# First scores in other banks, HGRN sums and logarithms pair by pair, exponentials behind the first eviction, one eviction by VectorE

## The reference, cut to what matters

```python
def hgrn2_mixer(q, i, g, zf, zb, lb, norm_g):
    ...
    o = (o_f + o_b).transpose(0, 2, 1, 3)
    gate = jax.nn.silu(g.astype(jnp.float32)).reshape(B, S, HG_HEADS, HEAD_DIM)
    o = rms_norm(o, norm_g) * gate
    return o.reshape(B, S, HG_WIDTH).astype(q.dtype)

    def attend(q_blk):
        s = jnp.einsum('bkgqd,bksd->bkgqs', q_blk, kh) * scale
        p = jax.nn.softmax(s, axis=-1)
        return jnp.einsum('bkgqs,bksd->bkgqd', p, vh)
```

## Time and profile before

| what | us |
|---|---|
| median of 3 runs | 1583.99 (1583.55 to 1588.25) |
| profiled execution | 1584.87 |
| its span, first to last instruction | 1583.0 |
| TensorE busy (matmul) in the span | 1532.4 (97%) |
| VectorE, ScalarE, GpSimd busy | 622.1, 424.9, 377.3 |
| chain that ended last: TensorE, DMA, VectorE, ScalarE | 81%, 9%, 7%, 2% |

### The profile page before, as it was taken

How to read it: one execution, slowest core, us unless ns; L and a number is a source line. 1 busy time by engine, 2 the same in 40 slices (tenths; PEclk the granted TensorE clock), 3 DMA queues, 4 the chain that set the end, 5 groups by cost and what they waited for, 6 DMA issues and landing times.

```text
span 1583.0 us, 20229 instructions
## 1 busy us (share of the span) xinstructions
PE 1532.4 (97%) x8166; PEld 786.7 (50%) x8166; DVE 622.1 (39%) x1244; ACT 424.9 (27%) x762; POOL 377.3 (24%) x432
## 2 busy tenths in 40 slices
PE   8999999999999999998999999999999999999986
PEld 4655566555444444443347546755554444444432
DVE  2687546462122212211427965464622122113114
ACT  3654651211111111111235547403111111111102
POOL 4671790000000000000265637700000000000004
PEclk9999999999999999999999999999999999999999
DMA  9300403699999999999950003066999999999997
GB/s 393 147 0 14 147 1 87 265 382 423 428 425 428 427 426 427 426 426 429 384 228 1 1 28 134 1 183 265 386 425 428 425 427 427 426 428 427 427 425 296
DMA packets 57682, 470.02 MB, mean 297 GB/s; under 512 B 19385, under 2 KB 19513, under 8 KB 29394
## 3 DMA queue, kind: packets, MB, share of 16 engines
q1 hardware_dynamic: 50338, 452.37, 69.0%
q0 software_dynamic: 7104, 16.24, 2.7%
q10 hardware_dynamic: 144, 0.07, 0.0%
HBM read 447.69 MB, written 26.74 MB: 300 GB/s over the span
## 4 chain that ended last, share of the span: by engine, by line
PE 81%; DMA 9%; DVE 7%; ACT 2%; issue 1%; POOL 0%; SPq 0%; POOLq 0%; DVEq 0%
PE bank L1035 24%; PE bank L1072 11%; PE bank L659 10%; PE bank L1025 9%; PE bank L817 6%; DMA ring<-wu 5%; DMA hbuf<-wu 2%; PE bank L738 2%; PE bank L725 2%; PE bank L753 2%; PE bank L651 2%; PE bank L1012 1%; PE bank L1059 1%; DVE x L2046 1%; PE bank L645 1%
## 5 line engine op out<-in xcount | busy, mean ns | idle before, releaser
L2268 POOL DMA_INDIRECT expert_rows<-raw_qd,store_rows x60 | 58.8, 979 | 999.4 <-ACT raw_qd L1472 939.3
L1035 PE MATMUL bank<-ring,hbuf 128*64 128x512 f32 x640 | 281.3, 593 | 5.3 <-DMA ring<-wu 5.3
L1036 PE MATMUL bank<-ring,hbuf 128*64 128x512 f32 x640 | 281.5, 593 | 0.0
L2020 DVE COPY raw_qd<-bank 128x256 f32<-128x256 f32 x64 | 27.2, 425 | 637.7 <-PE bank L1059 637.7
L659 PE MATMUL bank<-hbuf,ring 128*128 128x512 f32 x480 | 210.8, 595 | 2.8 <-DVE hbuf L1535 2.8
L1035 PEld LDWEIGHTS bank<-ring,hbuf 128*64 128x64 f32 x640 | 86.7, 137 | 184.2 <-issue 184.2
L1035 PE MATMUL bank<-raw_qd,hbuf 128*64 128x512 f32 x372 | 165.4, 597 | 3.9 <-DMA hbuf<-wu 3.9
L1072 PE MATMUL bank<-ring,raw_qd 128*64 128x512 f32 x352 | 160.4, 598 | 3.1 <-DVE raw_qd L2020 3.1
L1074 PE MATMUL bank<-ring,raw_qd 128*64 128x512 f32 x352 | 160.4, 598 | 0.0
L1025 PE MATMUL bank<-raw_qd,x 128*128 128x192 f32 x896 | 159.5, 332 | 0.0
L1465 ACT ACTIVATE raw_qd<-bank 64x512 f32<-64x512 f32 x64 | 37.8, 590 | 417.3 <-PE bank L1036 417.3
(11 more groups left out here) (405 smaller groups left out, 2233.8 us busy)
## 6 DMA issues: line engine op xcount, KB each, us to landing
ring<-wd SPq DMA_DIRECT2D x40, 2048.0 KB, 19.0
ring<-wg SPq DMA_DIRECT2D x38, 2048.0 KB, 19.1
ring<-wu SPq DMA_DIRECT2D x36, 2048.0 KB, 21.9
ninth_slot<-wd SPq DMA_DIRECT2D x20, 2048.0 KB, 20.4
hbuf<-wu SPq DMA_DIRECT2D x18, 2048.0 KB, 23.9
raw_qd<-wg SPq DMA_DIRECT2D x18, 2048.0 KB, 19.4
ring<-w_in SPq DMA_DIRECT2D x6, 2048.0 KB, 18.8
raw_qd<-wg SPq DMA_DIRECT2D x6, 1792.0 KB, 12.6
```

The costliest lines, as they stand in the source:

```text
L1035: mm(pb[2 + par][0:CAP, :], tokens[:, k, :], gates[k], start=(k == 0), stop=(k == KT - 1))
L1036: last = mm(pb[2 + par][CAP:P, :], tokens[:, k, :], ups[k], start=(k == 0), stop=(k == KT - 1))
L2268: G.indirect_dma_start(out=half_rows, out_offset=bass.IndirectOffsetOnAxis(ap=store_i[:, e:e + 1], axis=0), in_=y_sb[e % 2], in_offset=Non ...
```

## The change

- `S_BANK` becomes (2, 0): even units have their scores in banks 2 and 3, odd ones in 0 and 1; the first group of the output projection goes to bank 2. `scores(0)` no longer waits for the evacuation of groups 24 and 25; `scores(1)` does.
- TensorE's order becomes `scores(0)`, `scores(1)`, `head_sums(0)`, `hgrn_out(1)`, `scores(2)`, `head_sums(1)`; the loop's first iteration has no scores.
- `pair_out` signals the square and the copy each. ScalarE takes the first pair's logarithm ahead of `pair_out(1)`, the second one's behind it. `turned(0)` waits for one logarithm per bank.
- Both exponentials for the roots move behind the eviction of unit 0.
- Both `head_norm` stand in VectorE's u = 1. At the end of that iteration VectorE evicts the transposed probabilities of unit 1 in place of ScalarE.

```diff
-        S_BANK, T_BANK, A_BANK = (0, 2), 4, (pb[6], pb[7])
-        EARLY_BANK = [pb[0], pb[6]] + [pb[6 + n % 2] for n in range(2, 2 * NB)]
+        S_BANK, T_BANK, A_BANK = (2, 0), 4, (pb[6], pb[7])
+        EARLY_BANK = [pb[2], pb[6]] + [pb[6 + n % 2] for n in range(2, 2 * NB)]
...
             def head_sums(p):
-                pe.wait_ge(s["ho_s"], on("ho_s") + p + 1)
+                pe.wait_ge(s["ho_s"], on("ho_s") + 2 * p + 1)
+                pe.wait_ge(s["kv_e"], on("kv_e") + HG)
...
                 if u == 0:
+                    pe.wait_ge(s["r_ln"], on("r_ln") + 5)
+                    pe.wait_ge(s["r_done"], on("r_done") + 5)
+                elif u == 1:
                     wait_evacuated(pe, layer, NG - 2)
                     wait_evacuated(pe, layer, NG - 1)
-                    pe.wait_ge(s["r_ln"], on("r_ln") + 5)
-                    pe.wait_ge(s["r_done"], on("r_done") + 5)
...
                 if u == 0:
-                    pe.wait_ge(s["ho_s"], on("ho_s") + 2)
-                    pe.wait_ge(s["ho_r"], on("ho_r") + 1)
                     pe.wait_ge(s["hs_m"], on("hs_m") + HG)
                 else:
                     pe.wait_ge(s["pt_e"], on("pt_e") + u)
                 for i in range(2):
+                    if u == 0:
+                        pe.wait_ge(s["ho_r"], on("ho_r") + i + 1)
...
                 if u >= 2:
                     pe.wait_ge(s["o_b"], on("o_b") + u - 1)
+                elif u == 1:
+                    pe.wait_ge(s["ho_s"], on("ho_s") + 4)
...
             scores(0)
             scores(1)
+            head_sums(0)
             hgrn_out(1)
-            head_sums(0)
+            scores(2)
             head_sums(1)
...
             for u in range(NU):
-                if u + 2 < NU:
+                if 0 < u < NU - 2:
                     scores(u + 2)
...
             def pair_out(p):
                 act.wait_ge(s["ho"], on("ho") + p + 1)
-                A(o_rs[p], O_BANK[:, :], ACT.Square)
+                A(o_rs[p], O_BANK[:, :], ACT.Square).then_inc(s["ho_s"], 1)
                 A(o_sb[p], O_BANK[:, :], ACT.Copy).then_inc(s["ho_s"], 1)
 
-            def head_rstd():
-                for p in range(2):
-                    act.wait_ge(s["ho_m"], on("ho_m") + p + 1)
-                    ins = A(o_rs[p], M_BANK[p][:, :], ACT.Ln, bias=eps, scale=1.0 / HD)
-                ins.then_inc(s["ho_r"], 1)
-                act.wait_ge(s["ho_r"], on("ho_r") + 1)
+            def head_log(p):
+                act.wait_ge(s["ho_m"], on("ho_m") + p + 1)
+                A(o_rs[p], M_BANK[p][:, :], ACT.Ln, bias=eps, scale=1.0 / HD).then_inc(s["ho_r"], 1)
+
+            def head_roots():
+                act.wait_ge(s["ho_r"], on("ho_r") + 2)
                 for p in range(2):
                     A(o_rs[p], o_rs[p], ACT.Exp, scale=-0.5).then_inc(s["ho_r"], 1)
...
             probs(0)
             probs(1)
+            head_log(0)
             pair_out(1)
-            head_rstd()
+            head_log(1)
             for u in range(NU):
-                act.wait_ge(s["pt"], on("pt") + u + 1)
-                if u >= 2:
-                    act.wait_ge(s["pv"], on("pv") + u - 1)
-                A(pT_sb[u % 2], banks[:, T_BANK:T_BANK + 2, :], ACT.Copy).then_inc(s["pt_e"], 1)
+                if u != BY_VECTOR:
+                    act.wait_ge(s["pt"], on("pt") + u + 1)
+                    if u >= 2:
+                        act.wait_ge(s["pv"], on("pv") + u - 1)
+                    A(pT_sb[u % 2], banks[:, T_BANK:T_BANK + 2, :], ACT.Copy).then_inc(s["pt_e"], 1)
+                if u == 0:
+                    head_roots()
                 if u + 2 < NU:
                     probs(u + 2)
...
-                if u in (1, 2):
-                    head_norm(u - 1)
+                if u == 1:
+                    head_norm(0)
+                    head_norm(1)
                 if u >= 1:
                     unit_out(u - 1)
+                if u == BY_VECTOR:
+                    dve.wait_ge(s["pt"], on("pt") + u + 1)
+                    V.tensor_copy(pT_sb[u % 2], banks[:, T_BANK:T_BANK + 2, :]).then_inc(s["pt_e"], 1)
```

More of the change, by code:

```diff
@@ L278, in trunk @@
             kv_e="ACT: chunk k v evacuated, after the decay rows", state="DVE: chunk states",
-            ho="PE: HGRN outputs of a pair of heads", ho_s="ACT: HGRN output of a pair, its squares",
-            ho_m="PE: HGRN square sums", ho_r="ACT: HGRN logarithms of both pairs, then rstd of each", o_a="DVE: o_a of a pair",
+            ho="PE: HGRN outputs of a pair of heads", ho_s="ACT: squares of the HGRN output of a pair, the output",
+            ho_m="PE: HGRN square sums", ho_r="ACT: HGRN logarithms of each pair, then rstd of each", o_a="DVE: o_a of a pair",
             qk="PE: attention scores", mx="DVE: row maxima",
             ex="ACT: probabilities", pn="DVE: inverse sums of a unit", pt="PE: probabilities transposed",
-            pt_e="ACT: transposed probabilities evacuated", pv="PE: attention output of a unit, inverse sums by row",
+            pt_e="ACT, once DVE: transposed probabilities evacuated", pv="PE: attention output of a unit, inverse sums by row",
             pn_e="DVE: inverse sums by row evacuated", o_b="DVE: o_b of a unit", u5="u stored, loaded by chunk, then S5 chunk matrix loaded",
@@ L311, in trunk @@
             ev_a=15, prep=3, h_e=4, act=2, h_s=4, sig_e=4, h_l=4, h_f=4, q_copy=8, r_sq=5, ke_e=4,
-            kv_e=4, r_ln=5, r_rs=5, ho_s=2, ex=16, ho_r=3, pt_e=16, bt_e=4, ke=8, y5_e=1, gx=4, h2_a=4,
+            kv_e=4, r_ln=5, r_rs=5, ho_s=4, ex=16, ho_r=4, pt_e=16, bt_e=4, ke=8, y5_e=1, gx=4, h2_a=4,
             rlT_e=4, rms2=1, gx2=2, ev_d=13, dve=161, lb=3, h_k=4, q_silu=4, h_c=4, head=4, r_y=5, hs_m=4,
@@ L412, in trunk @@
         NU = QH // 2 * NB
+        BY_VECTOR = 1
         target = {8: Z[0], 9: Z[1], 10: Z[2], 11: Z[3], 12: hq[0], 13: hq[1], 16: ak,
@@ L685, in hgrn_kv @@
                 if hh == 2:
-                    pe.wait_ge(s["ho_s"], on("ho_s") + 1)
+                    pe.wait_ge(s["ho_s"], on("ho_s") + 2)
                 for b in range(NB):
@@ L795, in first_early @@
                 for k in tiles:
-                    last = mm(pb[0][:, :], mixed[k][:, 0:P], w_o[0][:, k, :], start=(k == 0), stop=(k == 5))
+                    last = mm(EARLY_BANK[0][:, :], mixed[k][:, 0:P], w_o[0][:, k, :], start=(k == 0), stop=(k == 5))
                 if tiles[-1] == 5:
@@ L1697, in head_norm @@
             def head_norm(p):
-                dve.wait_ge(s["ho_r"], on("ho_r") + p + 2)
+                dve.wait_ge(s["ho_r"], on("ho_r") + p + 3)
                 link(STT(out=o_sb[p], in0=o_sb[p], scalar=pcol("hgrn_g"), in1=o_rs[p], op0=ALU.mult, op1=ALU.mult))
```

## The result

The changed kernel took 1590.69 us in the median of 12 runs (1588.04 to 1594.1); the kernel before took 1584.97 beside it (12 runs, 1583.55 to 1588.25). The ratio is 1.0038, with a 95% interval from 1.003 to 1.0046: slower by 5.7 us. The forecast was 1586.6 with a range to 1589.4, so it is outside. The profiled execution took 1588.04, its span 1586.2, and is the fastest of the twelve. That matters: one trace is not the median here.

The account below looks back on a forecast made before the run. TensorE has no slack behind attention's start, so the start of unit 1's values decides in each of two layers. 2 x 1.3 = 2.6 on the median 1583.99 gives 1586.6 (+0.16%), range 1583.0 to 1589.4.

Parts of the forecast that it names:

- The wait that the prediction named as the one that decides: Values(1) waits for VectorE's eviction of turned(1), queued behind both norms: 1.28 later than before, taken as 1.3 a layer.
- The rule quoted from the Trainium skill: A flush behind each VectorE operation would make the four norm operations cost about 2.2 more, time near 1591; given no chance.
- The first: Rival: VectorE isn't late, probs(2) holds; scores(4) 0.43 earlier a layer, time 1583.1; chance 0.12.
- The tables (second): Rival: the square between the logarithms forces extra ScalarE table loads, 1.4 a layer more, time 1589.4; chance 0.08.
- The banks (third): Rival: first scores aren't released by the banks, so 0.73 a layer stays, time 1588.1; chance 0.04.
- stands idle for some 1.7: TensorE before scores(4), after scores(3), values(0) and turned(1) are done by 176.7; about 1.7 again before values(1).
- slower by over 0.3%: Outcome for the whole kernel, described as rival 2 and a little more; chance 0.10.

Follow-up runs that it names:

- The first two experiments: Changed kernel with unit 1's eviction back on ScalarE: 1584.56 us; changed kernel with the second head_norm back in unit 2, VectorE still evicting: 1584.82 us.
- the pair with the doubled copy: Changed kernel with VectorE's unit 1 copy done twice: 1593.53 us; the same plus 12 and 24 useless TensorE products in the two gaps: 1590.9 us.

## Why the prediction was wrong

**Right, within 0.1 us:** scores(0) 162.50 (162.51), sums(0) 164.42 (164.43), outputs(1) 165.47 (165.49), scores(2) 169.84 (169.91), sums(1) 170.89 (170.87), the second logarithm 172.06 (172.05), the first eviction 173.49 (173.55), probs(2) 176.89 (176.91), scores(4) 178.37 (178.40), the first norm 176.50, the copy 180.09 (180.17) and 1.21 long (1.22), values(1) 181.36 (181.44). Second half of turned(0): 172.80 against 172.94. The wait that the prediction named as the one that decides is the one that decides, and its price was right: 1.26 a layer against 1.3. The first two experiments show it from both sides, since without either VectorE's turn or the second norm's place the delay is gone.

**Right: VectorE without a flush.** The norm's second operation starts 0.03 after the end of the first (177.25, 177.28), the copy directly behind unit_out. The rule quoted from the Trainium skill ("VectorE: DVE Perf Modes", "The DRAIN you can't avoid") would have put values(1) 2.2 later than it is. The same section adds that a next operation that isn't held starts earlier, which the prediction left out. Its estimate of near 1591 lies next to the measured time, and for a reason that has nothing to do with it.

**Rivals.** The first needed an eviction that ends by 179.7; it ended at 181.30. The tables (second) cost nothing: two table loads in the stretch, as before. The banks (third) did what the diff says: no idle time at 162.50, and the kernel with the banks alone is not slower.

**The step that failed: TensorE's idle time was priced as its length.** The prediction wrote that TensorE "stands idle for some 1.7" before scores(4) and "again about 1.7 before values(1)", and took for each only the delay. It took the granted clock of the earlier trace rows, 1.00 throughout, for the changed kernel too. In the kernel before nothing like this pair was to be seen: at the start of attention TensorE has gaps of 0.73 and 0.60 and one of 0.67:

```profile
176.78 1.09 PE L753 MATMUL bank<-ring,raw_qd 128*64 128x128 f32 x16 [0.67 <-ACT ring L1383]
```

In the changed kernel there are 1.59 and 1.50 with 1.5 us of products between them, and in three of the four traced layers the clock falls to 0.50 in or just behind the second. By the mean clock that is at most (0.9967 - 0.9944) x 1588 = 3.7 us a run; by the table, in which 5.0 us go with 0.0048 of clock, it is 2.4. By the traces it is 1.7 to 2.8 for each layer in which it falls (70.13 and 70.26 against 68.42, and 71.21 against 68.42). The late values are 2.5 of the 5.7; the 3.2 left over lie within these bounds. That the rest is the clock and not more waits is shown by the pair with the doubled copy, where more work in the same waits was 2.6 faster, and by the table by clock. That it takes both gaps is likely, not shown: with one of 1.59 left the mean clock is nearly that of before, but with 0.68 and 1.73 it lies between.

**The range and the chances.** The clock was in no rival and in no bound. With a case for it, a fall in each layer in which TensorE, busy for 3.4 us at half its rate (964.8 to 968.2 above), loses half of that, it is 2 x (1.3 + 1.7) = 6.0, so 1584.0 + 6.0 = 1590: slower by over 0.3% at far more than 0.10.

**Open.** In the same kernel, with gaps equal within 0.1 us, one layer keeps its clock and the other doesn't; no run shows what selects. The clock also fell in the routing stage (near 328 to 331 us, or 1106 and 1116) in four of the profiles, the kernel with the banks alone among them, near 1520 us in three, before included, and at the very end in all. I don't lay that to the change, though the traces are too few to exclude it. It costs little: the second profile of the changed kernel has two such falls in the routing stage, and yet it takes 715.2 between the two attentions and 571.4 behind the second, against 715.4 and 571.6 before. And the filling of the gaps in the changed kernel itself raised the clock without gaining time, for which I have no account.

## What to carry to other kernels

Add up TensorE's idle time by place, not only in sum: here two waits of about 1.5 us close together cost some 3 us more over two layers than their length, and with one of them gone that came back. When an engine takes over work for another, look at what is queued ahead of that work: here the second norm, which nobody waited for, stood before the eviction that TensorE waited for, and moving it one unit on took away the whole loss of 6 us. With the roots and both norms moved it became a gain of 3.3. And check not only what a moved operation is queued ahead of, but also what the neighbouring engines do at that time: the norm that fell beside GpSimd's large operations cost 8 us.

## What the runs showed of the hardware

- **TensorE's clock after short gaps.** Where gaps of 1.58 to 1.59 and 1.45 to 1.77 us had 1.5 us of products between them, the granted clock fell to the 1.2 GHz level, in the second gap or up to 0.6 us behind it, in three of the four layers whose traces there are (of the changed kernel, profiled twice), for 3 to 7 us; products of 1.09 us took up to 1.98. After 1.59 alone, or 0.68 and 1.73, the profiles show no fall there. With useless products in the gaps neither profile has a fall in attention; the mean clock was 0.9976 in one kernel, the highest of all, and 0.9962 in the other.
- **VectorE beside GpSimd.** An operation of VectorE on two tensors in SBUF, 128x512, took 0.69 to 1.12 in all the traces of this stretch, where GpSimd has operations of 128x288 or nothing, and 3.66 to 4.45 beside its 128x2048 operation on two tensors. The maxima, which read PSUM, kept their 1.20 to 1.23 beside it. The Trainium skill ("GPSIMD Engine Reference", "Specifications") says that GpSimd shares its way to SBUF with VectorE and that instructions with two SBUF inputs contend; the trace agrees, and gives it a price of some four to six times.
- **VectorE reading two banks of PSUM.** A copy of 128x1024 took 1.21 to 1.23, as the maximum over the same size (1.20 to 1.23), against 1.00 to 1.03 for ScalarE's copy.
